# Two attention branches swap places in a software pipeline of sixteen steps

## The reference, cut to what matters

```python
def diff_attention(q, k, v, lq1, lk1, lq2, lk2, subln, lambda_init, cos, sin):
    ...
    lam = (jnp.exp(jnp.sum(lq1.astype(f32) * lk1.astype(f32)))
           - jnp.exp(jnp.sum(lq2.astype(f32) * lk2.astype(f32))) + lambda_init)
    ...
        p = jax.nn.softmax(logits, axis=-1)
        a = p[:, :, 0] - lam * p[:, :, 1]
        o = jnp.einsum('bhqs,bshd->bqhd', a.astype(v.dtype), v)
        o = rms_norm(o, subln) * (1.0 - lambda_init)
```

## Time and profile before

| | us |
|---|---|
| runs of the kernel before | 3854.52, 3857.18, 3855.15 (median 3855.15) |
| profiled execution, its own time | 3849.41 |
| its span | 3847.6 |
| PE busy, share of the span | 3453.1, 90% |
| DVE busy | 2575.6, 67% |
| ACT busy | 1791.8, 47% |
| mean granted clock of TensorE, as a share of full speed | 0.955 |
| the stage `attend` and the barrier behind it, first layer | 214.6 to 326.1 |
| the same, second layer | 1621.9 to 1732.4 |

### The profile page before, as it was taken

The page is one execution under the profiler, slowest core; times in us unless marked ns, Lnnn a source line. Parts: engine busy times, 40 slices in busy tenths (PEclk is TensorE's granted clock), DMA queues, the critical chain, the costliest instruction groups (busy, mean ns, idle before and its releaser), DMA issues. The chain is left out here.

```text
span 3847.6 us, 61859 instructions
## 1 busy us (share of the span) xinstructions
PE 3453.1 (90%) x19918; PEld 3000.1 (78%) x19918; DVE 2575.6 (67%) x5193; ACT 1791.8 (47%) x3301; POOL 69.3 (2%) x62
## 2 busy tenths in 40 slices
PE   4889889899999997789799899999969889898798
PEld 3767777788888886677687788888857789687697
DVE  5666569877777767574569777777766466545565
ACT  2344415855555553344328655555533345344354
POOL 0010000000000000010000000000000200000000
PEclk9989999999999998899899999999989899999999
DMA  6623522177777766315332377777744054453253
GB/s 226 226 63 112 178 100 92 62 233 237 238 245 244 238 203 205 114 48 175 129 123 72 115 247 236 237 247 244 237 154 142 6 198 169 143 189 113 89 181 115
DMA packets 271505, 637.17 MB, mean 166 GB/s; under 512 B 38911, under 2 KB 90647, under 8 KB 265198
## 3 DMA queue, kind: packets, MB, share of 16 engines
q1 hardware_dynamic: 233122, 561.56, 44.3%
q10 hardware_dynamic: 38220, 73.55, 5.6%
HBM read 633.89 MB, written 1.15 MB: 165 GB/s over the span
## 5 line engine op out<-in xcount | busy, mean ns | idle before, releaser
L147 PE MATMUL experts_ps_h<-uP_lo,experts_u_hi 128*128 128x256 f32 x1728 | 488.9, 283 | 0.0
L148 PE MATMUL experts_ps_h<-uP_hi,experts_u_lo 128*128 128x256 f32 x1728 | 488.9, 283 | 0.0
L146 PE MATMUL experts_ps_h<-uP_hi,experts_u_hi 128*128 128x256 f32 x1728 | 487.9, 282 | 0.0
L138 ACT ACTIVATE experts_u_hi<-kept 128x512 fp32r<-128x512 f32 x432 | 269.2, 631 | 354.2 <-PE experts_ps_h L148 351.3
L141 DVE TENSOR_TENSOR experts_v_lo<-u_w,experts_v_hi 128x512 fp32r<-128x512 f32 x432 | 299.0, 692 | 164.9 <-ACT experts_v_hi L138 161.8
L141 DVE TENSOR_TENSOR experts_u_lo<-kept,experts_u_hi 128x512 fp32r<-128x512 f32 x432 | 291.4, 689 | 153.9 <-ACT experts_u_hi L138 140.9
L138 ACT ACTIVATE experts_v_hi<-u_w 128x512 fp32r<-128x512 f32 x432 | 272.2, 630 | 204.0 <-PE expert_y L148 204.0
L146 PE MATMUL expert_y<-experts_v_hi,experts_w_hi 128*128 128x512 f32 x864 | 343.1, 397 | 1.1 <-DVE experts_w_lo L141 1.1
L147 PE MATMUL expert_y<-experts_v_lo,experts_w_hi 128*128 128x512 f32 x864 | 338.3, 392 | 0.0
L146 PEld LDWEIGHTS experts_ps_h<-uP_hi,experts_u_hi 128*128 128x128 f32 x1728 | 330.9, 191 | 8.4
L147 PEld LDWEIGHTS experts_ps_h<-uP_lo,experts_u_hi 128*128 128x128 f32 x1728 | 330.8, 191 | 8.4
(11 more groups left out here) (555 smaller groups left out, 8060.7 us busy)
## 6 DMA issues: line engine op xcount, KB each, us to landing
u_w<-in_peer_v SPq DMA_DIRECT2D x256, 512.0 KB, 4.3
kept<-in_peer_u SPq DMA_DIRECT2D x216, 512.0 KB, 4.3
kept<-in_ada_w_all ACTq DMA_DIRECT2D x140, 512.0 KB, 5.3
up_w<-in_ffn_w_up SPq DMA_DIRECT2D x44, 1024.0 KB, 5.8
od_in_w<-in_od_w_in SPq DMA_DIRECT2D x36, 1024.0 KB, 5.1
in_w<-in_w_in SPq DMA_DIRECT2D x48, 752.0 KB, 5.5
turns<-in_w_gate SPq DMA_DIRECT2D x32, 1024.0 KB, 5.2
down_w<-in_ffn_w_down SPq DMA_DIRECT2D x44, 512.0 KB, 3.7
```

What stands on the lines that cost most here:

```text
L138: return act.activation(self.hi[at], value, ACT.Copy)
L146: pe.matmul(out, left.hi[left_at], right.hi[right_at], start=start, stop=False, skip_group_check=skip)
L147: pe.matmul(out, left.hi[left_at], right.lo[right_at], start=False, stop=False, skip_group_check=skip)
L148: return pe.matmul(out, left.lo[left_at], right.hi[right_at], start=False, stop=stop, skip_group_check=skip)
```

## The change

The order of the first two branches in `KINDS` is swapped, and what hangs on their places follows: the norm of `diff` moves from slots 11 to 13 to slots 7 to 9, its late turns go to slots 10 and 11, and those of `mla` to 13 and 14 (`swa` stays in 17 and 18). The products of the lambdas move from DVE's slot 3 to slot 1, their exponential from ACT's slot 4 to slot 2, the rest from DVE's slot 5 to slot 3. SP's wait at line 848 asks for the weighing of steps 4 to 7 in place of 0 to 3, as its code counts by the place of `mla`.

```diff
-    KINDS = ("mla", "diff", "swa", "nat")
+    KINDS = ("diff", "mla", "swa", "nat")
     STEPS = [(k, h) for k in KINDS for h in (range(0, 8, 2) if k == "mla" else range(4))]
     NS, PER_KIND = len(STEPS), 4
 
     SCORES, EXPS, PROBS, WEIGH = 1, 2, 3, 4
-    DIFF_NORM = 2 * PER_KIND - 1 + WEIGH
-
-    LATE = {PER_KIND * (n + 1) + WEIGH + 1 + (n == 1) + b: (k, b) for n, k in enumerate(KINDS[:-1]) for b in range(TB)}
+    DIFF_NORM = PER_KIND - 1 + WEIGH
+
+    LATE = {PER_KIND * (n + 1) + WEIGH + 1 + (n == 0) + b: (k, b) for n, k in enumerate(KINDS[:-1]) for b in range(TB)}
...
-                    if i == PER_KIND:
+                    if i == EXPS:
                         act.wait_ge(lam_sum, 1)
                         act.activation(lexp[:], lsum[:], ACT.Exp).then_inc(lam_exp, 1)
...
                 def norm_diff():
-                    dve.wait_ge(out_done, 2 * PER_KIND)
+                    dve.wait_ge(out_done, PER_KIND)
...
-                    if i == PER_KIND - 1:
+                    if i == SCORES:
                         lambdas()
-                    if i == PER_KIND + 1:
+                    if i == PROBS:
                         lambda_rest()
```

## The result

The kernel after took 3836.53 us, the median of five runs (3834.18 to 3838.57), beside 3854.52 for the kernel before in the same comparison: ratio 0.9957, interval 0.9946 to 0.9968, or 12 to 21 us less. The forecast was 3847.7 with a range of 3840 to 3857. By the mark of the prediction, 7.7 us, this is a clear gain, to which it gave 0.44 beside 0.50 for no change. The profiled execution took 3836.53 (span 3834.7), 12.9 less than the one of before. One execution of experiment 7 took 6705.68 us beside 3827.47 to 3832.80 for its other three, and the ratios leave out such slow executions.

The account below looks back on a forecast made before the run. In the fill nothing is full, a chain of waits; from slot 5 PE works without a gap. Fill -20.0 plus slots 5 to 15 +12.5 gave -7.5: profiled 3849.4 to 3841.9, plus 5.7 to the median 3847.7, range 3840 to 3857.

Parts of the forecast that it names:

- the mark of the prediction: Whole time: a measurement can tell about 0.2%, 7.7 us, from no change.
- fill, slots 0 to 4: Step-by-step chain of waits from the first transpose; fill falls to 18.0 us, saving 10.7 and 9.3, together 20.0.
- slots 5 to 8: Latent work behind the fill: three slots of 5.3 and one of 4.9, 20.9 us against 17.3.
- The late turns: Slots 10, 11, 13, 14: all four have a turn behind waiting for DVE, one wait more than before.
- Rival 1: Clock stays up from offset 12 and in slots 11 and 14: 8.4 us less in all, 3839.3; chance 0.18.
- Slots 9 and 10: Transposes of slot 9 wait about 3.3 for DVE, slot 10's late turn for the scaling: 17.8 us against 16.0.
- The contention: POOL's pairs slow DVE's norm near slot 8: four operations wait 0.5 each, 2 us before the maxima.
- rival 3: Clock stays down in latent slots 5 to 8, 9.6 for 5.3; two such slots a layer give 3864.8; chance 0.06.
- rival 4: Scalars' wait and DVE's order hold slots 2 to 4 longer by 4 us a layer: 3855.7, same; chance 0.08.
- rival 2: POOL and DVE collide: seven norm and scaling operations each wait 1.27; at most half reaches PE, 3855, same; chance 0.11.
- the scaling untouched by POOL: DVE's scaling of diff, at offset 48, mostly escapes contention with POOL.
- SP: Merge loads wait for slot 11's weighing, about 63 us after the start against 62.5, with over 40 us spare: cost 0.

Follow-up runs that it names:

- experiment 7: Kernel after with diff's norm and scaling back in slots 11 to 13 and mla's late turns ahead of diff's: stages 202.4 us, ratio to kernel before 0.9946.
- Experiment 3: Kernel after with an extra 0.73 us DVE product ahead of the lower part in slots 10, 11, 13, 14: stages 224.6 us, ratio to kernel before 0.9996.
- experiment 4: Kernel after with all six late turns in slots 14 to 19: stages 196.6 us, ratio to kernel before 0.993.
- experiment 5: Kernel after with lambda products and their exponential one slot later: one execution, 3835.11 us, stages 203.3.
- experiment 2: Kernel after with POOL starting its pairs only behind diff's norm and scaling: stages 203.2 us, ratio to kernel before 0.9939.
- experiment 6: Kernel after with 32 unused PE transposes in slot 9 before its wait for DVE: stages 206.8 us, ratio to kernel before 0.997.
- experiment 11: Kernel after measured once more, unchanged: 3837.37 us, stages 208.5, ratio to kernel before 0.9963.
- experiment 8: Kernel after with late turns in slots 14 to 19, POOL behind diff's scaling, lambda loads ahead of masks and sink: 3813.04 us, ratio to kernel before 0.9904.
- the third edit: In experiment 8, the six small lambda loads issued ahead of masks and sink on SP; it had no run of its own.

## Why the prediction was off

Its terms, in its own order, layer 1 and 2:

| term | before | forecast | measured | error of the sum |
|---|---|---|---|---|
| fill, slots 0 to 4 | 28.7, 27.3 | 18.0 | 17.2, 16.9 | -1.9 |
| slots 5 to 8 | 17.3 | 20.9 | 20.6, 20.6 | -0.7 |
| slots 9 to 11 | | 17.8 + 8.1 = 25.9 | 27.2, 25.7 | +1.2 |
| slots 12 to 15 | | 5.1 + 6.4 + 7.4 + 4.9 = 23.8 | 21.5, 21.5 | -4.7 |
| slots 16 to the end | 18.65 | 18.65 | 18.5 | -0.3 |

Together -6.4: the stages fell by 13.9 where I had 7.5. Of the 11.2 us between forecast and median, this is 6.4. Another 5.7 is the step from the profiled execution to the median: I added 5.7 as the median of the kernel before stood that far above it, but the profiled execution of the kernel after was itself the median. Outside the stages the time grew by 1.0, which is the other way. The size of the gain thus carries an uncertainty of some 5 us that no term had. With every term of the stages exact the forecast would have been 3841.3, inside the range; that the number lies outside takes both errors.

**The step that failed is "The late turns".** For slot 12 I took 5.1 and for slot 15 4.9, and put slot 14 at 7.4, a mean between the clock levels. I priced them by their like before, where the lower level had come behind waits of 2.18 and 2.08. After, behind finish of a latent or windowed step, the waits were 1.50, as I had read it in the earlier trace rows at 302.63, and the transposes behind three of four in layer 1 (279.78: 0.30) and all in layer 2 are at the upper level. Slots 12, 14 and 15 took 4.30, 6.40 and 4.38. I had seen the shorter work and took it off the wait, but not off the chance of the clock. Slot 11, put at 8.1 with the lower clock, took 7.86 and 6.40. Rival 1, which had 0.18, named this, and is nearest: it has 15.9 less in the stages where 13.9 were measured. It was right for slot 14 and for slot 11 in layer 2, and not for the fill. Experiment 3 supports the mechanism and shows how close it was: 0.73 more in each such wait and layer 2 alone loses 13.9. That a wait of 1.50 leaves the level up is no rule, as experiment 4 shows. Over all the traces it held in 39 of 44 cases.

**The fill** went by the steps given: exponential at 6.7 (6 to 7), lambda sums at 8.2, second maxima at 8.8 (8.9). The scores of step 3 started at 13.0 and 12.7, for 12.2, and slot 4 then ran at the upper clock and ended 4.2 later in both layers, where I took the middle. The load bound it in layer 2 only (experiment 5). My reading of the clock of before was short: 0.70 of 28.7 us and 0.75 of 27.3 mean about 17 and 14 us at the lower level, not 5 to 10.

**Slots 9 and 10** were under-priced, 17.8 for 19.3 and 19.4. The contention was right in kind. It touched the norm's operations (0.29, 0.23 and 0.92 more) and two beside them, L1062 in finish (0.96) and L1047 in the maxima of slot 8 (0.71): 3.1 us for the 2 of the forecast. The wait was 3.85 for 3.3. The 16.0 that I took from slots 13 and 14 of before had the lower clock behind a wait of 2.09 in it. Behind 3.85 it came at once and stayed longer: the transposes, weighing, scores, transposes and weighing of slots 9 and 10 took 1.7 us more than those did. For this PE reached slot 10's late turn at 269.81, when DVE had nearly caught up, so the wait ahead of slot 11 was 1.50 (1.96 in layer 2) and not the 4 I forecast. The two errors cancel to 1.2 since both are the same lag of DVE; experiments 2 and 6 speed PE up and get 4.14 and 4.08 back at that place.

**The Trainium skill's rule** (GPSIMD Engine Reference, Key points: POOL contends with DVE instructions that are in a 2-port mode or have two inputs in SBUF) held: L1062, L1076, L1078 and L1047 were stretched, the sum of one input (L1077) stayed at 0.69, and experiment 2 removed all of it. L1062 and L1076 have two inputs in SBUF; in which mode the scalar L1078 and L1047 run, no run shows. Without this term the forecast would have come out 3.5 lower, nearer to the result, but by luck: the term is real, and it is the others that had the forecast too high.

**Right in full:** slots 5 to 8 at the upper clock (rival 3 falls, rival 4 with the fill, and rival 2 with a stretch of 3.1 and not of seven times 1.27); the scaling untouched by POOL, which was done at 260.9, 0.69 each at 264.07 to 266.94; and SP:

```profile
277.87 0.94 SPq L111 DMA_DIRECT2D turns<-in_w_gate  x2
```

It goes at offset 63.1 against 62.5, and costs nothing. **Wrong:** that nothing moves outside the stages by more than tenths. It moved by +3.3 and -2.6, and over all the kernels the stretch between stages took 1295.6 to 1301.2 and that behind them 2112.6 to 2119.7. For the one kernel that was traced twice they repeat (experiment 11), and they belong to no edit that I can name. Their cause is open. Both together go from 3411.0 to 3419.3, and these 8 us are the limit of what whole times tell here.

## What to carry to other kernels

Put the lightest work into a pipeline's fill, where each step waits for the one before it and the clock may be low; here a third of the gain could also be had by letting an engine serve the oldest step first. Before reordering branches, look at what waits for a shared PSUM tile: moving the late turns to where no turn follows gave as much as the whole swap (0.9961 beside 0.9957). Both together gave 0.993, and with POOL held back and the lambda loads first 0.9904. Where one engine lags, shortening a single wait moves it to the next meeting point; ask first which engine has the work, and price a wait by whether the clock falls behind it.

## What the hardware showed beyond that

- POOL is stretched as well as DVE: its sum of two inputs of 512 columns, alone 1.27, took 1.58 beside the norm, and its scalar operation 0.94 for 0.62. DVE's reduce of one input (0.69), reciprocals (0.16) and copy from PSUM (1.21) were not stretched.
- The price of this contention varies with no edit: the same instructions made slot 9 wait 3.85 and 3.84 in one trace of the kernel after, and 3.44 and 4.66 in the other.
- TensorE's level behind a wait is not told by the wait alone. In all thirteen traces, behind the fill, PE came from the upper level to 44 waits of 1.50 to 1.57, and the lower level followed 5 of them. It followed none of 7 waits of 1.63 to 1.96, 16 of 23 of 2.08 to 2.93, and all 20 of 3.21 to 4.67.
- Two edits that remove waits with a common cause can gain more together than apart: 21.9 us for three, of which two gave 11.5 and 4.9 alone. How much of the other 5.5 is the third edit, or the clock, is not shown; layer 2 of experiment 8 alone had 3.7 less than layer 1.
